# Three turns between blocks as pipelined stages, and tokens chosen by an index search

## The reference

```python
x = x + g1 * rms_norm(ml, norm1_post)                  # ml = merged @ w_out
h2 = rms_norm(x, norm2_pre) * (1 + sc2) + sh2
aff = softmax(h2 @ router)                             # 512 x 16
gate, idx = lax.top_k(swapaxes(aff, 1, 2), 64)         # 64 tokens for each expert
...
x = x + g2 * rms_norm(zeros.at[idx].add(ye * gate), norm2_post)
xm = _rms_norm(h, norm_mix_w) * (1 + scale_m) + shift_m
...
h = h + gate_m * (merged @ w_out_2)
xf = _rms_norm(h, norm_ffn_w) * (1 + scale_f) + shift_f   # then group and expert logits
```

## Time and profile before

| | us |
|---|---|
| median of 3 runs (lowest to highest) | 4228.22 (4227.66 to 4228.58) |
| the profiled execution | 4227.81 |
| its span, first to last instruction | 4225.5 |
| PE matmul busy in it | 3428.7 (81%) |
| DVE busy | 1546.8 (37%) |
| ACT busy | 916.8 (22%) |
| mean granted PE clock | 0.892 of full speed |

### The profile page before, as it was taken

How to read it: one execution, slowest core, us unless ns; L and a number is a source line. 1 busy time by engine, 2 the same in 40 slices (tenths; PEclk the granted TensorE clock), 3 DMA queues, 4 the chain that set the end, 5 groups by cost and what they waited for, 6 DMA issues and landing times. The chain is left out here.

```text
span 4225.5 us, 56473 instructions
## 1 busy us (share of the span) xinstructions
PE 3428.7 (81%) x23892; PEld 2063.1 (49%) x23892; DVE 1546.8 (37%) x3163; ACT 916.8 (22%) x1817; POOL 53.6 (1%) x72
## 2 busy tenths in 40 slices
PE   5799999998698988699748787848888887659994
PEld 1466666666555544344333232334444444358883
DVE  2466666666345756100140000031413233241112
ACT  1243344342134446100110000011111212001001
POOL 0000000000000000000000000000000000000000
PEclk7899999999799998799859999959899999859997
DMA  3112212221222211420149999340111110247873
GB/s 135 46 56 71 71 56 71 71 70 55 73 70 68 67 63 50 176 100 0 73 187 391 428 428 428 142 164 3 80 40 42 40 43 0 85 158 293 326 317 150
DMA packets 109172, 548.20 MB, mean 130 GB/s; under 512 B 34336, under 2 KB 37136, under 8 KB 84512
## 3 DMA queue, kind: packets, MB, share of 16 engines
q1 hardware_dynamic: 102048, 519.97, 31.9%
q0 software_dynamic: 4608, 16.78, 1.1%
q10 hardware_dynamic: 2304, 8.39, 0.5%
HBM read 517.63 MB, written 27.47 MB: 129 GB/s over the span
## 5 line engine op out<-in xcount | busy, mean ns | idle before, releaser
L2066 PE MATMUL ex_ps<-ex_ring,ex_xs 128*64 128x512 f32 x1024 | 246.7, 639 | 62.1 <-DMA ex_ring<-expert_slabs_in 59.1
L571 PE MATMUL rw_ps<-hT,rw_w 128*128 128x512 f32 (+1 forms) x640 | 259.4, 535 | 16.4 <-DMA rw_w<-rw_slabs_in 16.1
L2803 PEld LDWEIGHTS ge_ps<-ge_xeT,ge_ring 128*128 128x128 f32 x2048 | 233.0, 193 | 10.5 <-issue 10.5
L2803 PE MATMUL ge_ps<-ge_xeT,ge_ring 128*128 128x128 f32 x2048 | 233.2, 276 | 2.9 <-DVE ge_xeT L2861 2.9
L2300 PE MATMUL mh_ps<-mh_w,xmT 128*128 128x512 f32 x512 | 221.5, 593 | 8.6 <-ACT mh_sg L2323 8.6
L2066 PEld LDWEIGHTS ex_ps<-ex_ring,ex_xs 128*64 128x64 f32 x1024 | 88.4, 147 | 219.9 <-issue 219.9
L1375 PE MATMUL sg_ps<-hTp,sg_w 128*128 128x512 f32 x384 | 174.4, 608 | 8.5 <-DMA sg_par<-conv_pars_in 8.5
L571 PEld LDWEIGHTS rw_ps<-hT,rw_w 128*128 128x128 f32 x640 | 113.4, 193 | 100.1 <-issue 73.8
L2300 PEld LDWEIGHTS mh_ps<-mh_w,xmT 128*128 128x128 f32 x512 | 97.0, 190 | 132.5 <-issue 120.5
L2291 PE MATMUL mh_ps<-xmT,mh_w_ahead 128*128 128x512 f32 x256 | 120.8, 636 | 22.8 <-PEq L61 22.8
L2066 PE MATMUL ex_ps<-ex_ring,ex_hidT 128*64 128x512 f32 x512 | 118.5, 617 | 14.2 <-DMA ex_ring<-expert_slabs_in 13.1
(11 more groups left out here) (568 smaller groups left out, 5538.8 us busy)
## 6 DMA issues: line engine op xcount, KB each, us to landing
ex_ring<-expert_slabs_in SPq DMA_DIRECT2D x96, 2048.0 KB, 19.8
ge_ring<-expert_slabs_in SPq DMA_DIRECT2D x48, 2048.0 KB, 12.3
rw_mod_w<-mod_w_in SPq DMA_DIRECT2D x64, 384.0 KB, 4.1
rw_mod_w<-ada_in SPq DMA_DIRECT2D x64, 256.0 KB, 3.3
...
```

The lines of the kernel that those rows point to most:

```text
L571: mm = pe.matmul(where[j, part], w[:, k, P * j:P * j + P], tokens, start=k == 0, stop=k == KC - 1)
L2066: mm = pe.matmul(ps[halves[j], bank, :], src[:, k, halves[j]], ring[:, (n + j) % RING, k, :], start=k == 0, stop=k == KC - 1)
L2803: mm = pe.matmul(ps[:, 2 + 2 * (j % 2) + n, P * f:P * f + P], w[:, k, P * f:P * f + P], xeT[:, j, k, :], start=k == 0, stop=k == KC - 1)
```

## The change

A new function `settle` does each of the three turns in one stage. It goes by token tiles `t` and column halves `h` in the order `STEPS`; each product stays in PSUM until DVE has taken it from there; `x` stays in SBUF for the next norm, and is stored to DRAM beside that; turned and scaled tiles are made half by ACT, half by DVE; the narrow product (router, decays, routing) is made for each tile, and its result is the small tile `lg` that the next stage reads. PE's list in the diff shows where turns and narrow products stand between the wide ones. For the second turn the products are those of `scat` and `ye`, with no turning of `m`. `choose_tokens`, `gdn_decays` and `route` lose their narrow products. `choose_tokens` finds positions with MAX_INDEX in each round, turns positions and values (two 16-column turns), and writes `scat` by eight comparisons of a row of all positions with the chosen one, times the weight. The tables' stage is gone; `gdn_decays` issues their DMAs behind its own.

```diff
+def settle(nc, cst, source, rows, norm, x_in, x_out, cols, head, lg, xT=None, xn_dram=None):
+NTT, H, KB = SEQ // P, 2, 8
+STEPS = ((0, 0), (1, 0), (0, 1), (1, 1), (2, 0), (2, 1), (3, 0), (3, 1))
+step_of = {th: n for n, th in enumerate(STEPS)}
...
+        if m is not None:
+            sp.dma_start(w[:, 0, :, :], slabs[0]).then_inc(w_in[0], 16)
+        sp.dma_start(gate[:, :], gate_row.broadcast_to([P, D])).then_inc(s.rows_in, 16)
+        if norm_row is not None:
+            sp.dma_start(row[:, :], norm_row.broadcast_to([P, D])).then_inc(s.rows_in, 16)
+        sp.dma_start(x[:, :, :], x_in.rearrange("(t p) d -> p t d", p=P)).then_inc(s.x_in, 16)
+        if m is not None:
+            sp.dma_start(w[:, 1, :, :], slabs[1]).then_inc(w_in[1], 16)
+        sp.dma_start(g[:, :], gain).then_inc(s.cols_in, 16)
+        sp.dma_start(sc[:, :], sc_col, allow_slow_non_contiguous=True).then_inc(s.cols_in, 16)
+        sp.dma_start(sh, sh_col, allow_slow_non_contiguous=True).then_inc(s.cols_in, 16)
+        for t in range(NTT):
+            sp.wait_ge(s.summed, H * t + H)
+            sp.dma_start(x_out[tile(t), :], x[:, t, :]).then_inc(s.x_stored, 16)
+            if xn_dram is not None:
+                sp.wait_ge(s.normed, t + 1)
+                sp.dma_start(xn_dram[tile(t), :], xn[:, t % 2, :]).then_inc(xn_stored[t % 2], 16)
+        sp.wait_ge(s.x_stored, 16 * NTT)
+        if xn_dram is not None:
+            for stored in xn_stored:
+                sp.wait_ge(stored, 8 * NTT)
...
+        def product(n, ks):
+            t, h = STEPS[n]
+            if m is not None and ks[0] == 0:
+                pe.wait_ge(s.mT_by_dve, t + 1)
+                pe.wait_ge(s.mT_by_act, t + 1)
+                pe.wait_ge(w_in[h], 16)
+            if t >= 2 and ks[0] == 0:
+                pe.wait_ge(s.taken, H * (t - 2) + h + 1)
+            for k in ks:
+                mm = pe.matmul(ps[:, ybank(t, h), :], left[:, k, tile(t)], right(k, h), start=k == 0, stop=k == KB - 1)
+            if ks[-1] == KB - 1:
+                mm.then_inc(s.product, 1)
...
+            pe.wait_ge(s.normed, t + 1)
...
+                mm = pe.transpose(ps[:, 4 + k // 4, tile(k % 4)], xn[:, t % 2, tile(k)], cst("ident"))
+                if k % 4 == 3:
+                    mm.then_inc(s.turned, 1)
...
+            pe.wait_ge(s.xT_by_act, t + 1)
+            pe.wait_ge(s.xT_by_dve, t + 1)
...
+            for k in range(KC):
+                mm = pe.matmul(ps[:, 6, NL * t:NL * t + NL], xT[:, k, tile(t)], hw[:, k, :], start=k == 0, stop=k == KC - 1)
+            mm.then_inc(s.logits, 1)
...
+                    mm = pe.transpose(ps[:, 2 * t + k // 4, tile(k % 4)], m[:, t, tile(k)], cst("ident"))
+                mm.then_inc(s.m_turned, 1)
+        for n in range(5):
+            product(n, every)
+        turn(0)
+        product(5, every)
+        turn(1)
+        logits(0)
+        product(6, every)
+        logits(1)
+        product(7, every[:4])
+        turn(2)
+        product(7, every[4:])
+        logits(2)
+        turn(3)
+        logits(3)
...
+        def square_y(t, h):
+            if norm_row is None:
+                return
+            act.wait_ge(s.product, step_of[t, h] + 1)
+            if step_of[t, h]:
+                act.wait_ge(s.y_squared, step_of[t, h])
+            act.activation(sq[:, 0, :], ps[:, ybank(t, h), :], ACT.Square, accum_out=ssy[:, t, h:h + 1]).then_inc(s.y_squared, 1)
...
+            for h in range(H):
+                act.wait_ge(s.summed, H * t + h + 1)
+                if t or h:
+                    act.wait_ge(s.x_squared, H * t + h)
+                act.activation(sq[:, 1, :], x[:, t, half(h)], ACT.Square, accum_out=ssx[:, t, h:h + 1]).then_inc(s.x_squared, 1)
+            act.wait_ge(s.mean_x, t + 1)
+            act.activation(rx[:, t:t + 1], rx[:, t:t + 1], ACT.Sqrt).then_inc(s.root_x, 1)
...
+        def keep_xT(t):
+            act.wait_ge(s.turned, H * t + 1)
+            for k in range(4):
+                ins = act.activation(xT[:, k, tile(t)], ps[:, 4, tile(k)], ACT.Identity, bias=sh[:, k:k + 1], scale=a[:, k:k + 1])
+            ins.then_inc(s.xT_by_act, 1)
...
+        square_y(0, 0)
+        square_y(1, 0)
+        square_y(0, 1)
+        root_y(0)
+        root_x(0)
+        square_y(1, 1)
+        root_y(1)
+        root_x(1)
+        square_y(2, 0)
+        keep_xT(0)
+        square_y(2, 1)
+        root_y(2)
+        keep_xT(1)
+        root_x(2)
+        square_y(3, 0)
+        keep_xT(2)
+        square_y(3, 1)
+        root_y(3)
+        root_x(3)
+        keep_xT(3)
...
```

DVE's list:

```diff
+        def add_y(t):
+            if norm_row is not None:
+                mean(ry, ssy, t, s.y_squared, [step_of[t, h] + 1 for h in range(H)]).then_inc(s.mean_y, 1)
+                dve.wait_ge(s.root_y, t + 1)
+                link(dve.reciprocal(ry[:, t:t + 1], ry[:, t:t + 1]))
+            if t == 0:
+                dve.wait_ge(s.x_in, 16)
+            for h in range(H):
+                y = ps[:, ybank(t, h), :]
+                if t:
+                    dve.wait_ge(s.summed, H * t + h - 1)
+                if norm_row is not None:
+                    dve.scalar_tensor_tensor(tmp[:, h, :], y, ry[:, t:t + 1], gate[:, half(h)], ALU.mult, ALU.mult).then_inc(s.taken, 1)
+                else:
+                    dve.wait_ge(s.product, step_of[t, h] + 1)
+                    dve.tensor_tensor(tmp[:, h, :], y, gate[:, half(h)], ALU.mult).then_inc(s.taken, 1)
+                dve.wait_ge(s.taken, H * t + h + 1)
+                dve.tensor_tensor(x[:, t, half(h)], x[:, t, half(h)], tmp[:, h, :], ALU.add).then_inc(s.summed, 1)
...
+        def norm_x(t):
+            mean(rx, ssx, t, s.x_squared, [H * t + 1, H * t + 2]).then_inc(s.mean_x, 1)
...
+            if t >= 2:
+                dve.wait_ge(s.turned, H * (t - 1))
+                if xn_dram is not None:
+                    dve.wait_ge(xn_stored[t % 2], 16 * (t // 2))
+            dve.tensor_scalar(xn[:, t % 2, :], x[:, t, :], rx[:, t:t + 1], None, ALU.mult).then_inc(s.normed, 1)
...
+        def keep_xT(t):
+            dve.wait_ge(s.turned, H * t + 2)
+            for k in range(4, 8):
+                ins = dve.tensor_scalar(xT[:, k, tile(t)], ps[:, 5, tile(k - 4)], a[:, k:k + 1], sh[:, k:k + 1], ALU.mult, ALU.add)
+            ins.then_inc(s.xT_by_dve, 1)
...
+        dve.wait_ge(s.cols_in, 48)
+        link(dve.tensor_scalar(sc[:, :], sc[:, :], 1.0, None, ALU.add))
+        dve.tensor_tensor(a, sc[:, :], g[:, :], ALU.mult).then_inc(s.a_ready, 1)
+        dve.wait_ge(s.a_ready, 1)
+        add_y(0)
+        norm_x(0)
+        add_y(1)
+        norm_x(1)
+        keep_xT(0)
+        add_y(2)
+        keep_xT(1)
+        norm_x(2)
+        keep_xT(2)
+        add_y(3)
+        norm_x(3)
+        keep_xT(3)
+        dve.wait_ge(s.logits, NTT)
```

In `choose_tokens`, `gdn_decays` and `route`:

```diff
-                sp.dma_start(w[:, :, :], router).then_inc(s.w_in, 16)
-                sp.dma_start(xn_dram.rearrange("(t p) d -> p t d", p=P), xn).then_inc(s.xn_stored, 16)
+        sp.dma_start(every[:, :], positions.broadcast_to([P, SEQ])).then_inc(s.every_in, 16)
+        for n in range(6):
+            sp.dma_start(ring[:, n, :, :], w_slabs[n]).then_inc(s.ring_in, 16)
+        sp.wait_ge(s.ring_in, 16 * 6)
...
+        pe.wait_ge(s.ranked, 1)
+        for n in range(2):
+            mm = pe.transpose(ps[:, 1, NE * n:NE * n + NE], best[:, n, :, :].rearrange("e j c -> e (j c)"), ident[0:NE, 0:NE])
+        mm.then_inc(s.best_turned, 1)
...
+        link(dve.tensor_reduce(st[:, 0, :], lg, AX.X, ALU.max))
...
+        for n in range(ROUNDS):
+            top, now = best[:, 1, 0, 8 * n:8 * n + 8], affT[:, n % 2, :]
+            link(dve.max(top, now))
+            link(dve.max_index(at[:, 8 * n:8 * n + 8], top, now))
+            if n + 1 < ROUNDS:
+                link(dve.match_replace(affT[:, (n + 1) % 2, :], top, now, -1.0))
+        link(dve.tensor_copy(best[:, 0, :, :], per_unit(at[:, :], 2)))
+        dve.tensor_copy(best[:, 1, 1, :], best[:, 1, 0, :]).then_inc(s.ranked, 1)
+        dve.wait_ge(s.best_turned, 1)
+        for j in range(2):
+            mine = ps[64 * j:64 * j + 64, 1, 0:2 * NE].rearrange("p (n g j) -> p n g j", n=2, j=2)[:, :, :, j]
+            link(dve.tensor_copy(place[64 * j:64 * j + 64, :, :], mine))
+        link(dve.tensor_copy(idx, place[:, 0, :]))
+        dve.wait_ge(s.every_in, 16)
+        for g in range(PAIRS_E):
+            dve.tensor_scalar(scat[:, g, :], every[:, :], place[:, 0, g:g + 1], place[:, 1, g:g + 1], ALU.is_equal, ALU.mult)
...
 # gdn_decays
-                sp.dma_start(w[:, :, :], ab_slab).then_inc(s.w_in, 16)
                 sp.dma_start(bias[:, :], dt_bias.broadcast_to([P, H])).then_inc(s.rows_in, 16)
...
+                for table, src in tables:
+                    sp.dma_start(table, src).then_inc(s.tables_in, 16)
                 sp.wait_ge(s.ahead_in, 32)
+                sp.wait_ge(s.tables_in, 48)
...
-                dve.wait_ge(s.beta, 1)
 # route
```

(9 more changed lines are left out.)

270 lines of the change are left out of this document (99 added, 171 removed).

## The result

The changed kernel takes 4072.95 us (median of 4 runs, 4071.1 to 4075.96) against 4227.94 (4226.31 to 4228.58). The ratio is 0.9635, with a 95% interval of 0.9618 to 0.9651: 155 us faster. Predicted were 4084, with a range from 4070 to 4108. Five more runs of the same kernel gave 4073.06 (ratio 0.9636, 0.9623 to 0.9649), with single runs from 4069.95 to 4077.52.

A forecast was written before the change was run, and what follows sets the result against it. TensorE, busy 81% of the span, was taken to lose time at three turns between blocks, where engines work one after another. Savings 29.3 + 26.3 + 35.3 + 9.3 + 30.6 + 13.3 = 144.1 us off 4227.8 gave 4084, range 4070 to 4108.

The forecast's parts named there:

- The middle of the stages: Between the wide products of each `settle`: three turns of a tile and two narrow products add 6.25 us, without stalls.
- The clock: In each `settle`: a third of one fall from 2.4 to 1.2 GHz, counted as 1 us a stage.
- Rival 1: Clock falls after each of three narrow runs in every `settle`: 27 us less 3 counted, 4108; chance 0.12.
- The tail: From the last wide piece to the next stage: 14.0 us plus 0.75; in the third turn 11.0 plus 0.75.
- First turn: First wide product to the choice's stage: 2118.1 against 2147.41, 29.3 us less.
- Choice: `choose_tokens` to first gather: ended by the ring's loads at 31.8, 33.3 against 59.6 us, 26.3 less.
- Second turn: Second turn's first product to `gdn_decays`: product's end plus 7.25 and 14.75, 2766.1 against 2801.44, 35.3 us less.
- `gdn_decays`: Stage ahead of the mixer: the tables' loads end last, 17.3 us with the join against 26.7, 9.3 less.
- 2: In `choose_tokens` the index search outlasts the ring's loads; at four passes, 3.0 us each, 4096; chance 0.04.
- 3: In `settle` hand-offs don't overlap, TensorE stands 6.6 us at each of turns 0 to 2: 4143; chance 0.04.
- 4: TensorE stays at 1.2 GHz through all three `settle` stages, 182 us: 4263, slower than before; chance 0.01.
- rival 5: Experts, bound by their loads, give back the choice's gain; without those 26 us 4110; chance 0.03.

The follow-up runs named there:

- `change_again`: The changed kernel run again with no edit, as base of the other runs: median 4073.06 us.
- experiment 6: Against the changed kernel, the second `settle` also issues the loads of `gdn_decays`, which then issues none: median 4068.70 us.
- `ring_four`: Against the changed kernel, `choose_tokens` loads four of the six ring slabs and `choice_experts` issues the other two first: median 4075.52 us.

## Why the prediction was right

11 us too high, in the range: 7.7 between the forecast of the profiled execution (4083.7) and what that took (4075.96), and 3.4 because the median of the changed kernel lies 3.0 below its profiled execution, where 0.4 above was taken. The chains of the stages were right, and what bounds each. That the six stretches of the sum came to 143.9 us against 144.1 is luck all the same: the errors of the stretches, 4.0, -3.3, 1.1, -2.6 and 0.7, cancel. By its steps:

- **The middle of the stages.** 6.25 us for turns and narrow products between the wide ones: measured 6.2 (61.37 against 55.17). Right in all three, less a slow start of 1.7 us in the third. Not one wait of TensorE in there, as said.
- **The clock.** A third of a fall for each stage, 1 us: none came between the wide products. Falls did come where the narrow products were tripled. Rival 1 (12% chance) is out here, though its mechanism exists. The rule by which turns don't engage the upper clock (the Trainium skill, "TensorE: Matmul & The Clock Gate", Part 4) would have given 4099; the granted clock was 1.00 in every window with a turn between products, and a turn of eight took 1.04 us against 1.97 behind a pause. Nor did the turns count as a pause: the clock rose from 0.50 to 1.00 while TensorE did nothing but the 32 turns of `m` (2028.54 to 2033.89 in the changed kernel), as these two windows show. The measurement decides against the rule for these fp32 turns. The trace doesn't name a transpose mode; a turn is one record in it where an fp32 product of the same size is two.

```profile
2030.60:2031.60 1.00, 1.00 (x7) 1.00 (x6) 0.17 (x1) 0.06 (x1) 0.00 (x0) 0.50 0.90 360
...
2032.60:2033.40 0.80, 0.80 (x10) 0.80 (x8) 0.35 (x1) 0.35 (x1) 0.00 (x0) 1.00 1.13 471
```

- **The tail**, 14.75 with the join and 11.75 in the third turn: measured 14.81 and 14.76, and 11.2 to 12.0. It was put together from rows of before; the error is under 0.1 us in the first two. Its low clock for the last turn and product was right too.
- **First turn, 29.3 against 33.3.** The mis-sized term is the 7.25 us: the wide products of before had begun with a fall worth 3 us, the changed kernel's didn't in this run; with `change_again`'s 64.18 in its place the gain would be 30.5. The other 1 us is the clock term. So of the 33.3 us 2.8 are luck of the run.
- **Choice, 26.3 against 23.0.** MAX_INDEX at 0.78 with its link and DVE's end at 26.7 were right, and that the ring decides. The two terms that failed are the end of the traffic (31.8, measured 33.2: it starts at 153 GB/s for 3 us) and the way from there to the gather (1.5, measured 3.4). I had the 1.5 from a stage that DVE ended; behind this stage, which a DMA ends, it was some 3 us in each profile. DVE idles for the last 9.8 us of the stretch, not 5.
- **Second turn, 35.3 against 36.4**: the clock term that wasn't needed.
- **`gdn_decays`, 9.3 against 6.7.** That the tables end it was right. Again the loads' slow start (50 GB/s until 4.4 us into the stage) and the join: 17.7 and 2.3 instead of 16.1 and 1.2. That nothing else holds it is shown by experiment 6.

```profile
2703.00:2706.00 3.00, 0.00 (x0) 0.00 (x0) 0.00 (x0) 1.38 (x2) 0.00 (x0) 0.50 0.33 50
...
2718.00:2719.00 1.00, 0.00 (x0) 0.00 (x0) 0.00 (x0) 0.00 (x0) 0.00 (x0) 0.50 0.92 369
2719.00:2720.00 1.00, 0.00 (x0) 0.00 (x0) 0.00 (x0) 0.00 (x0) 0.00 (x0) 0.50 0.18 64
```

- **Third turn and `route`**, 30.6 and 13.3: measured 31.3 and 13.3.
- **Not in the sum**: 6.4 us of the experts' phase, of which 4.8 are the run (rate and clock) and 1.6 stay open, and 1 to 2 us up and down elsewhere. Since the errors above cancel, these stretches, taken as unchanged, make up the whole of the 7.4 us between 144.1 and 151.5.
- **The rivals.** 2 fell by 0.75 us a search; 3, since no wait stands between the products; 4 as well, the clock was 1.00 in nearly all of the stages; and 5, because the gather starts the experts as before, 9.5 us behind it, and the gain arrived. The mechanism of rival 5 exists nevertheless: `ring_four` lost its 8 us in just this place.
